# A two-layer hybrid encoder: probabilities times V in 32 bit floats, the sample as 128 columns, a new tile order, and GpSimd adding the indexer's scores of two tiles

## The reference

```python
z = rmsnorm(x) @ w_in                      # q 512, k 128, v 128, indexer q 256, indexer k 32, wi 8, u 512, gv 512
score = sum over 8 heads of relu(qi @ ki.T) * wi   # chunk-causal; the best 128 keys of a row are kept (sample: 48)
a = softmax(q @ k.T / 8 over the kept keys) @ v    # 8 heads of 64, 2 key/value heads
gvn = rmsnorm(gelu(gv)) * gate_norm
b = gelu(u) * (w_spatial @ gvn + b_spatial)        # 8 groups, chunks of 128 positions
x = x + concat([a, b]) @ w_out
x = x + (relu(rmsnorm(x) @ w1) ** 2) @ w2          # hidden width 4096
```

## Time and profile before

| What | Value |
|---|---|
| median of 3 runs | 1423.07 us |
| profiled execution, its own time | 1424.25 us |
| its span, first to last instruction | 1422.4 us |
| TensorE busy | 1327.7 us |
| VectorE busy | 700.4 us |
| ScalarE busy | 533.8 us |
| GpSimd busy | 244.1 us |
| mean granted TensorE clock | 0.971 |

### The profile page before, as it was taken

The page is one execution under the profiler, slowest core; times in us unless marked ns, Lnnn a source line. Parts: engine busy times, 40 slices in busy tenths (PEclk is TensorE's granted clock), DMA queues, the critical chain, the costliest instruction groups (busy, mean ns, idle before and its releaser), DMA issues.

```text
span 1422.4 us, 23791 instructions
## 1 busy us (share of the span) xinstructions
PE 1327.7 (93%) x9993; PEld 1288.4 (91%) x9993; DVE 700.4 (49%) x1304; ACT 533.8 (38%) x988; POOL 244.1 (17%) x259
## 2 busy tenths in 40 slices
PE   5988688999999999999999786989999999999997
PEld 5977577999999999999998775879999999999997
DVE  2387933445434444444648675435544444443443
ACT  6466285333223123133336546624321322322322
POOL 3264255110000000000224623522000000000011
PEclk8899899999999999999999888999999999999999
DMA  6111012232222323232421111114232232323221
GB/s 176 45 46 33 28 30 60 68 89 78 87 80 85 89 75 90 77 87 75 120 61 45 46 30 30 30 31 127 75 89 79 86 88 76 87 78 89 75 75 67
DMA packets 177963, 102.46 MB, mean 72 GB/s; under 512 B 7433, under 2 KB 176321, under 8 KB 177857
## 3 DMA queue, kind: packets, MB, share of 16 engines
q1 hardware_dynamic: 177856, 100.95, 24.6%
HBM read 96.98 MB, written 3.95 MB: 71 GB/s over the span
## 4 chain that ended last, share of the span: by engine, by line
PE 84%; ACT 5%; DVE 5%; POOL 3%; issue 2%; DMA 1%; SPq 0%; POOLq 0%; ACTq 0%; DVEq 0%
PE bank L1660 65%; PE bank L1406 11%; PE bank L1564 2%; PE bank L1538 1%; POOL late L609 1%; DVE m L1110 1%; PE bank L1518 1%; DVE late L1112 1%; ACT pl_a L852 1%; POOL ssacc L546 1%; DVE vl L1212 1%; PE bank L1471 1%; ACT p_hi L863 1%; DMA late<-in_x_prompt 1%; PE bank L1587 1%
## 5 line engine op out<-in xcount | busy, mean ns | idle before, releaser
L699 ACT ACTIVATE ring_hi<-ring_raw 128x1024 fp32r<-128x1024 f32 x176 | 184.7, 1050 | 267.1 <-PE bank L1660 248.7
L1660 PE MATMUL bank<-vh,ring_hi 128*128 128x288 f32 x1280 | 275.6, 297 | 3.5 <-DVE vl L1212 3.5
L1660 PE MATMUL bank<-vh,ring_lo 128*128 128x288 f32 x1280 | 275.2, 296 | 0.0
L1660 PE MATMUL bank<-vl,ring_hi 128*128 128x288 f32 x1280 | 275.2, 296 | 0.0
L991 DVE TENSOR_TENSOR ring_lo<-ring_raw,ring_hi 128x1024 fp32r<-128x1024 f32 x150 | 193.5, 1291 | 67.5 <-ACT ring_hi L699 60.5
L1660 PE MATMUL bank<-xh,ring_hi 128*128 128x288 f32 x1024 | 220.7, 297 | 1.9 <-issue 1.9
L1660 PE MATMUL bank<-xl,ring_hi 128*128 128x288 f32 x1024 | 220.2, 296 | 0.0
L1660 PE MATMUL bank<-xh,ring_lo 128*128 128x288 f32 x1024 | 220.1, 296 | 0.0
L1660 PEld LDWEIGHTS bank<-vh,ring_hi 128*128 128x128 f32 x1280 | 205.1, 188 | 4.5 <-DVE vl L1212 4.4
L1660 PEld LDWEIGHTS bank<-vl,ring_hi 128*128 128x128 f32 x1280 | 205.4, 188 | 0.0
L1660 PEld LDWEIGHTS bank<-vh,ring_lo 128*128 128x128 f32 x1280 | 205.1, 188 | 0.0
(11 more groups left out here) (195 smaller groups left out, 1641.9 us busy)
## 6 DMA issues: line engine op xcount, KB each, us to landing
ring_raw<-in_w_ff SPq DMA_DIRECT2D x128, 512.0 KB, 3.8
ring_raw<-in_w_in SPq DMA_DIRECT2D x32, 512.0 KB, 3.7
ring_raw<-in_w_out SPq DMA_DIRECT2D x32, 128.0 KB, 2.9
ring_raw<-in_w_out SPq DMA_DIRECT2D x16, 256.0 KB, 3.1
late<-in_x_prompt SPq DMA_DIRECT2D x4, 512.0 KB, 5.6
out_y_prompt<-late SPq DMA_DIRECT2D x4, 512.0 KB, 2.7
w_sp<-in_w_spatial SPq DMA_DIRECT2D x2, 512.0 KB, 4.6
gate_bc<-in_gate_norm SPq DMA_DIRECT2D x2, 256.0 KB, 5.5
```

Source lines behind the costliest of these rows:

```text
L699: s.activation(ring_hi[:, n % NSLOT, :], ring_raw[:, n % NRAW, :], ACT.Copy).then_inc(hi_ready, 1)
L1660: last = mm(bank[unit_bank(u) + half][:, 0:HALF], w[:, k, :], a[:, k, HALVES[half]], start=k == 0 and w is wh and a is ah, stop=k == KT - ...
```

## The change

- **Sample tile.** `xh` is widened by 64 columns that hold the sample's low part; `feed` writes them in stages 0 and 2 with a second operation. A sample half sum takes these 128 columns (64 high, 64 low) against high and low weights: two matmuls for a slice of K in place of three. The result's lower 64 partitions are scaled by ScalarE (`s_part`), and VectorE adds the upper 64 (`sample_sum`, two slots after the tile's end, `s_evac`). Whoever needs the sample's rows, or its bank, waits for `s_evac`.
- **Probabilities times V** in 32 bit floats: one copy `p_t` (three buffers) by ScalarE for steps below `NSV` = 13, by VectorE from there; v is read from `z` and `cache_v`; each head's product writes its own 64 partitions with 256 columns. Output banks 6 and 7 alternate; the transposes have bank 5 alone. `out_high` and `out_low` are one operation each. `v_hi` and `v_lo` go.
- **Order.** Tiles run 0, 1, sample, 2, 3 in all of the attention part. Small columns, indexer and its transposes stand about two slots earlier, the transposes of q three later, the first logits four later, the last steps one earlier. Three of the five spatial products move to slots 80 to 82. The spatial weights are transposed first and copied by ScalarE. END is 84.
- **Scores.** `NXV = 2 * NIH`: ScalarE scales and GpSimd adds for tiles 2 and 3. `FILL` is changed.
- **Gate.** VectorE takes squares and the scaling with gate_norm in one operation each; ScalarE keeps the gelu, GpSimd has no gain step.
- **First sums of squares.** VectorE squares and sums the input rows as they arrive (`row_square`); ScalarE's squares, GpSimd's adds and the row sums of layer 0 go. Layer 1 has its row sums in slot 2.
- **GpSimd's order.** A slot's weight split stands before the rotary steps and adds. The split for unit 1 moves from slot 78 to 79, so it stands behind `gated` (slot 78), as that of unit 2 did.
- The loads of caches, spatial weights and gate_norm come after the second chunk's weights.

```diff
-    NXV = 3 * NIH
+    NXV = 2 * NIH
-    ORDER = [(0, 0), (1, 0), (0, 1), (1, 1), (2, 0), (3, 0), (SMP, 0), (2, 1), (3, 1), (SMP, 1)]
+    ORDER = [(0, 0), (1, 0), (SMP, 0), (0, 1), (1, 1), (SMP, 1), (2, 0), (3, 0), (2, 1), (3, 1)]
+    TURN = TILE_ORDER
...
-        return NP * c + (NT - 1 if c == 0 else ORDER.index((SMP, 0)))
+        return NP * c + (NT - 1 if c == 0 else ORDER.index((NPT - 1, 0)))
...
-    SUMS_AT, SMALL_AT, TURN_AT = 6, 7, 9
+    SUMS_AT, SMALL_AT, SMALL_ROWS_AT = 2, 6, 7
+    SUM_AT = {ended(c, SMP) + 2: c for c in range(NC)}
-    TR_AT = {14: [0, 1], 15: [2, 3], 24: [4], 26: [5], 28: [6], 31: [7]}
-    QUAD_AT = {17: 0, 19: 1, 21: 2, 23: 3, 25: 4, 27: 5, 30: 6, 33: 7}
-    SCORED = dict(zip(INDEX_TILES, [21, 25, 29, 40]))
+    TR_AT = {9: [0], 10: [1], 12: [2, 3], 13: [4, 5], 24: [6], 26: [7]}
+    QUAD_AT = {15: 0, 17: 1, 19: 2, 21: 3, 23: 4, 26: 5, 28: 6, 31: 7}
+    SCORED = dict(zip(INDEX_TILES, [19, 23, 27, 44]))
-    Q_ROPE_AT = {30: (0, 0, NPT), 31: (0, SMP, NT), 35: (1, 0, 2), 40: (1, 2, NPT), 41: (1, SMP, NT)}
-    QT_AT = {38: 0, 39: 1, 43: 2, 44: 3, 45: 4}
-    QK_AT = [41, 43, 45, 47, 49, 54, 56, 58, 60, 67, 69, 71, 73]
+    Q_ROPE_AT = {25: (0, 0, 2), 31: (0, 2, NPT), 34: (0, SMP, NT), 35: (1, 0, 2), 39: (1, SMP, NT), 40: (1, 2, NPT)}
+    QT_AT = {41: 0, 42: 1, 45: 2, 46: 3, 47: 4}
+    QK_AT = [45, 47, 49, 51, 53, 58, 59, 61, 63, 66, 68, 70, 72]
-    GELU_AT = {61: [0, 1, 2], 62: [3, 4]}
-    MEAN_AT, ROOT_AT = 64, 65
-    MIX_AT = {70: 0, 71: 1, 72: 2, 73: 3, 74: 4}
-    MIX_BANK = [5, 6, 5, 6, 7]
+    GELU_AT = {64: TURN}
+    SQUARE_AT = {65: TURN}
+    MEAN_AT, ROOT_AT = 66, 66
+    SCALE_AT = {68: [0, 1], 70: [SMP, 2, 3]}
+    MIX_AT = {74: 0, 77: 1, 80: 2, 81: 3, 82: 4}
+    MIX_BANK = [3, 4, 3, 4, 3]
-    T_BANK = [5 + k % 2 for k in range(NS)]
-    FILL = [(0, 0), (21, 2), (34, 3), (41, 2), (50, 3), (67, 0)]
+    T_BANKS = [5]
+    T_BANK = [T_BANKS[k % len(T_BANKS)] for k in range(NS)]
+    O_BANK = [6 + g % 2 for g in range(NGR)]
+    FILL = [(0, 0), (19, 2), (31, 4), (43, 1), (48, 2), (57, 2), (67, 0)]
...
+                if stage % 2 == 0:
+                    last = v.scalar_tensor_tensor(xh[:, j, TOK:TOK + DEC], x[:, j, SEQ:TOK], gain(stage, j),
+                                                  xh[:, j, SEQ:TOK].bitcast(F32), ALU.mult, ALU.subtract)
...
+            def row_square(t):
+                dve.wait_ge(x_in_ready[t], 16)
...
+                v.tensor_tensor_reduce(out=pl_a[0:ROWS[t], 2 * (t % 2):2 * (t % 2) + 2, :].rearrange("p a n -> p (a n)"),
+                                       in0=rows, in1=rows, scale=1.0 / D, scalar=EPS, op0=ALU.mult, op1=ALU.add,
+                                       accum_out=ms[0:ROWS[t], t:t + 1]).then_inc(first_squares, 1)
...
+                def sample_sum(c):
+                    src, rr = bank[proj_bank(c, SMP)][DEC:2 * DEC, 0:CW], r[0:DEC, SMP:SMP + 1]
...
+                    dve.wait_ge(s_part, NC * l + c + 1)
+                    v.scalar_tensor_tensor(target(c, SMP), src, rr, target(c, SMP), ALU.mult, ALU.add).then_inc(s_evac, 1)
...
+                            if t == SMP:
+                                for w_ in w:
+                                    last = mm(bank[b][:, 0:CW], xh[:, kx, SEQ:TOK + DEC], w_[:, kx % KH, :],
+                                              start=kx == 0 and w_ is w[0], stop=kx == KT - 1 and w_ is w[1])
+                                continue
...
-                    for w, p in ((v_hi, p_hi), (v_lo, p_hi), (v_hi, p_lo)):
-                        last = mm(bank[7][:, 0:GQA * ROWS[t]], w[0:n, block, :], p[0:n, k % 2, 0:GQA * ROWS[t]],
-                                  start=b == 0 and w is v_hi and p is p_hi, stop=b == BLOCKS[a] - 1 and p is p_lo)
+                    for kv in range(NKV):
+                        last = mm(bank[O_BANK[g]][HD * kv:HD * kv + HD, 0:w2], vals[:, HD * kv:HD * kv + HD],
+                                  p_t[0:n, k % 3, kv * w2:(kv + 1) * w2], start=b == 0, stop=b == BLOCKS[a] - 1)
```

More of the change, by code:

```diff
@@ L733, in _ @@
             for j in range(KT):
-                s.activation(xh[:, j, :], x[:, j, :], ACT.Copy, scale=gain(0, j)).then_inc(xh_ready, 1)
+                s.activation(xh[:, j, 0:TOK], x[:, j, :], ACT.Copy, scale=gain(0, j)).then_inc(xh_ready, 1)
             split_hi(1)
-            split_hi(2)
-            for j in range(KT):
-                feed(j, 0)
             for l in range(DEPTH):
@@ L760, in evac @@
+                    if c in (Q0, Q1):
                         src = src.rearrange("p (b d) -> p b d", d=HD)
[L761 to L767 removed]
+                    if c in (U0, U1) and t != SMP and ended(c, t) + 1 > U_GELU_AT:
+                        func = ACT.Gelu_apprx_tanh
@@ L934, in _ @@
                         s.activation(rv[:, :], rv[:, :], ACT.Sqrt).then_inc(root_ready, 1)
-                    for t in SCALE_AT.get(at, ()):
-                        gating_scale(t)
                     if at == U_GELU_AT:
-                        for t in range(NT):
+                        for t in TURN:
                             u_rows_gelu(t)
@@ L1015, in _ @@
             dve.wait_ge(g_ready, 1)
+            link(v.memset(ms[:, :], 1.0))
+            for t in range(2):
+                row_square(t)
             split_lo(0)
+            for t in range(2, NT):
+                row_square(t)
+            dve.wait_ge(first_squares, NT)
+            v.reciprocal(r[:, :], ms[:, :]).then_inc(ms_ready, 1)
             for j in range(KT):
@@ L1166, in masked_logits, with gate_square, gate_scale @@
                                            accum_out=nmax[0:rows, i:i + 1]).then_inc(masked, 1)
+                def gate_square(t):
+                    m, rows = TURN.index(t), gvn[0:ROWS[t], t, :]
+                    dve.wait_ge(gv_gelu, NT * l + m + 1)
+                    if m:
+                        dve.wait_ge(gv_sq, NT * l + m)
+                    v.tensor_tensor_reduce(out=gsq[0:ROWS[t], :], in0=rows, in1=rows, scale=1.0 / DB, scalar=EPS,
+                                           op0=ALU.mult, op1=ALU.add, accum_out=mv[0:ROWS[t], t:t + 1]).then_inc(gv_sq, 1)
+                def gate_scale(t):
+                    rows = ROWS[t]
+                    dve.wait_ge(rv_ready, l + 1)
+                    dve.wait_ge(small_in, 16 * 5 * (l + 1))
+                    v.scalar_tensor_tensor(gvn[0:rows, t, :], gvn[0:rows, t, :], rv[0:rows, t:t + 1], gate_bc[0:rows, :],
+                                           ALU.mult, ALU.mult).then_inc(gvn_ready, 1)
                 def mix_copy(m):
@@ L1276, in _ @@
                             out_low(g)
+                    for t in SCALE_AT.get(at, ()):
+                        gate_scale(t)
                     if at - 1 in MIX_AT:
@@ L1450, in _ @@
                 zz = lambda t, a, b: z[0:ROWS[t], t, a:b]
-                tr_parts = [[ki4[:, t, :] for t in range(NPT)],
+                tr_parts = [[w_sp[:, 4 * n + g, :] for g in range(4)] for n in range(2)]
+                tr_parts += [[ki4[:, t, :] for t in range(NPT)],
                             [cache_ki4[:, :, :].rearrange("p a d -> p (a d)"), ki4[0:DEC, SMP, :]]]
@@ L1455, in _ @@
                              [cache_k[:, :], zz(SMP, Z_K, Z_K + DKV)]]
-                tr_parts += [[w_sp[:, 4 * n + g, :] for g in range(4)] for n in range(2)]
                 def small_columns():
@@ L1530, in p_transpose @@
                         pe.wait_ge(q_lo_ready, NT * (l + 1))
[L1531 to L1536 removed]
+                    if k >= len(T_BANKS):
+                        pe.wait_ge(p_copied, NS * l + k - len(T_BANKS) + 1)
                     for j, i in enumerate(GROUP[g]):
@@ L1605, in _ @@
                         half_sum(at)
-                    if at == SUMS_AT:
+                    if l and at == SUMS_AT:
                         row_sums(l)
@@ L1668, in _ @@
                 pe.wait_ge(al_ready, NGR * (l + 1))
-                pe.wait_ge(p_lo_ready, NS * (l + 1))
+                pe.wait_ge(p_copied, NS * (l + 1))
                 unit(0, attn)
-                for t in range(NT):
-                    mt_group(t)
+                for a in range(NT):
+                    mt_group(a)
                 pe.wait_ge(vl_ready, (NT + FT) * l + 1)
```

315 lines of the change are left out of this document (144 added, 171 removed).

## The result

The changed kernel takes 1346.57 us (median of 4, 1345.16 to 1347.40) against 1422.84 for the kernel before beside it: a ratio of 0.9464, 95% interval 0.9448 to 0.9480. Forecast were 1362.0 (1338 to 1386). The direction and the range held; the sum, -60.8 us, was 18.3 short of the -79.1 between the two profiled executions (1424.25 and 1345.16).

What follows compares the result with a forecast made beforehand. The prediction took TensorE, busy for 93% of the span, to bound the kernel, with its gaps in the attention parts. Its terms summed to -60.8 us from 1424.25, giving 1363.4, or 1362 as the median, with a range of 1338 to 1386.

Steps and rivals of the forecast that it cites:

- the first sums: Start of layer 0: squares move to VectorE, so TensorE's wait, small products and a slow half sum go; -9.8 us.
- contention: Gate squares and scaling on VectorE beside GpSimd: one 2 us delay a layer on the copies' way; +4 us.
- rival A: Probabilities times V: the two halves of V run at once; -17 us, total 1345, chance 0.20.
- the price of probabilities times V: 40 large steps at 0.86 us, taken from the spatial product, in place of 0.70: +6.4 us, ends -10.8 and +14.4.
- The step that failed in the clock: Attention parts: some 15 us lost to TensorE's lowered clock; without the long waits, less new loss, -10 us.
- (a): Top-k of tile 2 no longer ends in a burst, by GpSimd's adds, four steps a slot, later slot: 16.4 us goes.
- (c): Before probabilities times V: one copy and two output banks cut 28.3 us of waits to about 6, the gelu's.
- (b): First transposes come two slots after the last q instead of one: 6.2 us of waiting goes.
- (d): End of the attention part: three spatial products fill the gaps, so 3.5 us of waiting becomes 0.6.
- New waits: Unit 1 behind GpSimd's gating +3.9 us a layer; with q transposes, index products and smaller ones, together +11.3.
- B: Middle of the attention part: VectorE comes to bound, up to 10 us a layer go to TensorE; 1382 us, chance 0.15.
- C: Probabilities times V: transposes' one bank delays every one of 48 steps, 1.4 us each; 67 us, total 1429, chance 0.05.

Runs made afterwards that it cites:

- nxv24: Changed kernel with the scores of tile 2 added up by VectorE again instead of GpSimd, the rest as it is: 1340.98 us, ratio 0.9413.
- old_fill: nxv24 with the earlier top-k steps a slot from slot 34 on (3, 2, 3) in place of 4 from 31, 1, 2: 1350.34 us, ratio 0.9474.

## Why the prediction was right, and where it was not

From TensorE's first record to its last there are 1413.7 us before and 1334.1 after. Going from record to record in the trace, this splits into time without a record (waits), half of the working time at a granted clock of 0.50 (lost to the clock), and the rest (work at 2.4 GHz). Each is one execution, and the clock differs between executions (means of 0.987 to 0.992 in four of the changed kernel). The forecast's terms, sorted the same way:

| Both layers, us | Forecast | Before to after | Measured |
|---|---|---|---|
| waits (-36.4 net, -6.1 of the first sums, +4 contention) | -38.5 | 86.2 to 40.5 | -45.7 |
| work (-15.0, +6.4, -1.1 of the first sums) | -9.7 | 1297.0 to 1283.0 | -14.0 |
| clock (-10, -2.5 of the first sums) | -12.5 | 30.5 to 10.6 | -19.9 |
| sum | -60.7 | 1413.7 to 1334.1 | -79.6 |

Each class came out larger than forecast and none with another sign, so the range held; the time is where rival A's is, but not for A's reason alone.

**The step that failed in the work** is the price of probabilities times V: "I take 0.86, since its shape is the same and no row shows two column halves at once". The columns streamed are the same, the operand's width isn't: 128*128 there, 128*64 here, and two of the latter run at once. Counted from end to end, as in the chain, and at full clock, the 48 steps took 36.3 us and take 26.2. But each makes its neighbour slower: transposes behind it take 0.59 in place of 0.44, a half sum 1.62 in place of 1.43, a spatial product 1.06 in place of 0.86 (as it did before behind logits products). Transposes grew by 3.5 in sum, spatial products by 0.4, and half sums of full tiles by 4.3. Only some 1.2 of the 4.3 is this border (38 half sums in place of 32 stand behind a narrower operand); most of the rest is a rise far from these steps too, from 1.417 to 1.439 behind another half sum, for which no run shows a cause. So the term is about -5 in place of +6.4, or -2 with all of the rise put on it. Rival A had the mechanism at a chance of 0.20; its step of 0.43 leaves out what each pair takes beside its columns and the border, and its -17 against the forecast was too much. The sample gave 13.5 of its 15.0: its half sums went from 1.40 to 0.95 us.

**The step that failed in the clock** is its base: I took two stretches and two ends of the attention parts, some 15 us lost in work. Those held 16.3, so their size was right, but there were 30.5: 3.6 at the start of layer 0, 3.3 from 33 to 43 us (the first sums' 2.5 lie there), 1.7 from 108 to 112, 2.3 from 791 to 798 and 3.3 at the kernel's end were left out. The mean clock of 0.971 over the span, in the page's table, says 41 us with the waits. Its other side was not foreseen: 4.6 of the 10.6 us that are still lost fall on the units after the new wait, where the forecast counted the wait alone. The 3.3 at the end stay as 2.8.

**Waits that go.** For those of the earlier trace rows behind the start and the index products' 2.4 the forecast was 66.3 to 29.9 us, the tables say 66.3 to 27.2. The sizes came out, two reasons did not. (a) said that GpSimd's taking over eight adds a layer helps top-k: nxv24 shows that it costs 6 to 7 us. It makes GpSimd late for a weight split; I counted its chain up to the q transposes and not the splits between. The places of the top-k steps, four a slot from 31, named beside it, were right (old_fill). Nor is the wait gone: 3.8 us, behind VectorE's gate work. (c) named two copies and one bank; the bank alone does little, the second copy alone 19 us, and the wait that the table names needs both. Of the gelu 2.9 us are left, 6 were forecast. (b) and (d), 6.2 and 3.5 us, are as forecast.

**New waits.** At unit 1 the step was right: +4.1 us a layer against +3.9, with the split right behind gating. GpSimd's hold on the q transposes became 0.8 us there and 4.4 on a split, 5.2 together in place of 8.4. Index products and their chain came to 7.7 in place of 5.9.

**Contention.** +4 was forecast as 2 us a layer on the copies' way. It sits where it was put, at the gate scaling, with 1.4 us of waiting a layer.

**The other rivals.** B, VectorE bounding the middle: no wait on the sample's sum above 0.4 us. C, the transposes' one bank: 2.9 us, only at the gelu; it becomes real with a second copy. Of the signs, waits on masked logits reach 1.4 us and not 1, and the stretch from slot 46 to the first unit is 31.5 and 35.3 us shorter and not 20.

## What to carry to other kernels

Price a matmul by the part of the array that its operand fills as well as by its columns, and by what it does to the work behind it: two that fill different halves cost as one if they stand next to each other, and the next full one starts later. A wait's row names who came last, not why; putting causes back one by one and together shows which of them the wait belongs to, and that a cause can cost 1 us by itself and 17 beside another. Where the bounding engine waits for a few us, look at the clock behind the wait too, and at moving the late work to an idle engine before shortening anything else.

## Not expected of the hardware

- A product of 256 columns with a 128*64 operand takes 0.58 us alone and 0.58 us with a second one beside it.
- Work with a 128*128 operand behind one of 64 rows or columns pays a border: 12 matmuls take 1.43 us behind transposes of 128x128 and 1.62 to 1.63 behind logits products (64*128), transposes of 64 rows or a product with V.
- 36 transposes and twice 28 products for nothing made the kernel 6 us faster by the ratio (4 by the medians), by the clock at three places.
